# Mixture-of-experts results scattered by choice and token, the last two blocks added through TensorE, routing and mLSTM head mixing regrouped, in a two-model kernel on one core

## The reference

```
wmat = (q @ k^T) * exp(dmat - m_t)
num = wmat @ v + s_inter * (q @ c_st)
den = sum(wmat) + s_inter * (q @ n_st)
h = num / maximum(abs(den), floor)
```

```
for n in range(32):
    a, b = jnp.split(h @ w_up[n], 2, axis=-1)
    out = out + combine[:, n:n + 1] * ((jax.nn.silu(a) * b) @ w_down[n])
return x + out
```

## Time and profile before

| | |
|---|---|
| median of 3 runs | 2659.19 us |
| profiled execution | 2661.43 us, span 2659.4 us |
| PE busy | 2503.9 us (94%) |
| DVE busy | 1586.5 us (60%) |
| ACT busy | 1142.9 us (43%) |
| POOL busy | 235.2 us (9%) |
| head mixing | 457.9 to 534 us of the span |
| routing | about 2296 to 2312 us |
| expert blocks | 2312 to 2632.4 us, 32 blocks |
| combining | 2632.4 to 2659.4 us |

### The profile page before, as it was taken

The page is one execution under the profiler, slowest core; times in us unless marked ns, Lnnn a source line. Parts: engine busy times, 40 slices in busy tenths (PEclk is TensorE's granted clock), DMA queues, the critical chain, the costliest instruction groups (busy, mean ns, idle before and its releaser), DMA issues. The chain is left out here.

```text
span 2659.4 us, 32240 instructions
## 1 busy us (share of the span) xinstructions
PE 2503.9 (94%) x11395; PEld 1911.9 (72%) x11395; DVE 1586.5 (60%) x2344; ACT 1142.9 (43%) x1882; POOL 235.2 (9%) x239
## 2 busy tenths in 40 slices
PE   8999997699999999999999999999899999899995
PEld 6877785577888886766788888678757777666663
DVE  6766435645555535644555553547899645588884
ACT  5432332334444325623444442433332532377773
POOL 0000001000000000000000000355324000211111
PEclk9999999999999999999999999999999999799997
DMA  4321232032333321202333332323102013499995
GB/s 149 111 80 64 95 111 79 1 143 79 95 95 95 126 96 65 81 32 86 94 96 100 100 127 71 108 79 112 66 33 95 1 64 123 160 354 378 387 386 208
DMA packets 196719, 320.64 MB, mean 121 GB/s; under 512 B 16513, under 2 KB 112673, under 8 KB 196609
## 3 DMA queue, kind: packets, MB, share of 16 engines
q1 hardware_dynamic: 191678, 310.71, 33.8%
q0 software_dynamic: 4736, 8.40, 1.0%
q10 hardware_dynamic: 195, 0.06, 0.0%
HBM read 298.43 MB, written 29.10 MB: 123 GB/s over the span
## 5 line engine op out<-in xcount | busy, mean ns | idle before, releaser
L399 PE MATMUL ps<-ffn_parts 128*128 128x512 f32 x1056 | 411.6, 390 | 2.5 <-DVE ffn_parts L394 1.7
L401 PE MATMUL ps<-ffn_parts 128*128 128x512 f32 x1056 | 410.9, 389 | 0.0
L400 PE MATMUL ps<-ffn_parts 128*128 128x512 f32 x1056 | 410.8, 389 | 0.0
L399 PEld LDWEIGHTS ps<-ffn_parts 128*128 128x128 f32 x1056 | 198.2, 188 | 46.6 <-issue 2.6
L394 DVE TENSOR_TENSOR ffn_parts<-ring,ffn_parts 128x1024 fp32r<-128x1024 f32 x132 | 157.8, 1223 | 120.5 <-ACT ffn_parts L2437 107.4
L401 PEld LDWEIGHTS ps<-ffn_parts 128*128 128x128 f32 x1056 | 198.2, 188 | 41.2
L400 PEld LDWEIGHTS ps<-ffn_parts 128*128 128x128 f32 x1056 | 198.3, 188 | 40.9
L394 POOL TENSOR_TENSOR w_lo<-ring,w_hi 128x512 fp32r<-128x512 f32 (+1 forms) x112 | 159.9, 1432 | 721.1 <-ACT w_hi L558 720.8
L2488 DVE SCALAR_TENSOR_TENSOR y_tmp<-ps,pcol,y_tmp 128x511 f32<-128x511 f32 x88 | 61.9, 745 | 211.4 <-ACT y_tmp L2421 211.4
L1012 ACT CAST front_w_hi<-ring 128x512 fp32r<-128x512 f32 x104 | 64.1, 620 | 212.3 <-PE ps L401 212.2
L394 DVE TENSOR_TENSOR front_w_lo<-ring,front_w_hi 128x512 fp32r<-128x512 f32 x104 | 71.5, 689 | 129.8 <-ACT front_w_hi L1012 129.6
(11 more groups left out here) (669 smaller groups left out, 5638.7 us busy)
## 6 DMA issues: line engine op xcount, KB each, us to landing
ring<-in_w_up SPq DMA_DIRECT2D x32, 1536.0 KB, 8.8
ring<-in_ffn_w_up SPq DMA_DIRECT2D x88, 512.0 KB, 4.8
moe_down<-in_w_down SPq DMA_DIRECT2D x32, 1024.0 KB, 9.7
ring<-in_ab_w_in SPq DMA_DIRECT2D x13, 2048.0 KB, 7.9
ring<-in_w_in SPq DMA_DIRECT2D x11, 2048.0 KB, 7.8
ring<-in_ffn_w_down SPq DMA_DIRECT2D x10, 2048.0 KB, 7.7
ring<-in_w_up SPq DMA_DIRECT2D x32, 512.0 KB, 9.5
ring<-in_c_w_in SPq DMA_DIRECT2D x6, 2048.0 KB, 8.0
```

The lines of the kernel that those rows point to most:

```text
L399: nc.tensor.matmul(out, left[0], right[0], start=start, stop=False, **more)
L400: nc.tensor.matmul(out, left[0], right[1], start=False, stop=False, **more)
L401: return nc.tensor.matmul(out, left[1], right[0], start=False, stop=stop, **more)
```

## The change

**Head mixing.** Each direction gets two banks of its own (banks 0 and 1 for the first, 2 and 3 for the second), scores move to bank 4, and `SI` has one bank (5) instead of two. `sums` and `read_out` now work on one unit (4 chunks) and not on a head. The second direction's `read_out` adds directly into hm with four scalar_tensor_tensor of 128x128. DVE's order changes to prepare(n+1), finish(n-1).

**Routing.** DVE makes the rests of the first up block itself (before, POOL made two of three), ahead of `layout`; PE turns and multiplies block 0 before it waits for `placed`; there are more fill passes (1 more ahead, 1 before `tokens`, 5 before turn_rows(0), 2 before first(0)). POOL gathers blocks 0 to 3 before its other work. A second table, `result`, is computed like `token` (8 more small matmuls twice): for each row of a block, in which row of a 1024-row DRAM tensor `results_of_choices` (choice * 512 + token) its result belongs.

**Results.** SP's stores are gone. POOL scatters each block's results by an indirect DMA to their places (`hand_out`), except those of the last two blocks. While these two run, SP loads the 1024 rows back as 8 plain DMAs of 512 KB into the weights' ring, once POOL says it is free (`free_ring`). `slots_of_last` on DVE, `turn_shares` on PE and a copy on ACT make a table of shares by row of the last two blocks; `mixed` multiplies it with their results, 16 whole matmuls of 96x128 by 512, and DVE adds that and the loaded rows to x. The block end between the two parts, and `combine`, are gone. `rows_and_shares` is replaced by `shares_of_blocks`, after step 3.

The core of the diff (PE, ACT and DVE get the steps named above in their last two steps; left out with the tables' code):

```
             def mix(n):
                 h, d = units[n]
                 pe.wait_ge(*k.vb(n + 1))
-                if d == 0 and h >= 1:
-                    pe.wait_ge(*k.da(h))
+                if n >= 2:
+                    pe.wait_ge(*k.da(n - 1))
...
-            def read_out(h):
-                dve.wait_ge(*k.sb(h + 1))
...
+                dve.wait_ge(*k.sb(n + 1))
...
+                if d == 0:
+                    for tiles, values in nums(d):
+                        last = nc.vector.tensor_tensor(b.parts[:, tiles, :], values[:, :, 0:ML_D],
+                                                       spread(rden[:, tiles].rearrange("p (e o) -> p e o", o=1), [P, tiles.stop - tiles.start, ML_D]), ALU.mult)
+                else:
+                    for c in range(NT):
+                        last = nc.vector.scalar_tensor_tensor(out=hm[:, c, h * ML_D:(h + 1) * ML_D], in0=num(c, d)[:, 0:ML_D], scalar=rden[:, c:c + 1],
+                                                              in1=b.parts[:, c, :], op0=ALU.mult, op1=ALU.add)
+                last.then_inc(k.da.sem, 1)
                 dve.drain()
-                nc.vector.tensor_tensor(hm[:, :, h * ML_D:(h + 1) * ML_D], b.parts[:, 0:NT, :], b.parts[:, NT:2 * NT, :], ALU.add)
...
+            def finish(n):
+                h, d = units[n]
+                read_out(n)
+                if d == 1:
+                    gate(h)
+                    if h >= 1:
+                        mean(h - 1)
...
-            for n, (h, d) in enumerate(units):
+            for n in range(len(units)):
                 if n + 1 < len(units):
                     prepare(n + 1)
-                if d == 1:
-                    read_out(h)
-                    if h >= 1:
-                        mean(h - 1)
-                    dve.drain()
-                    gate(h)
+                if n >= 1:
+                    finish(n - 1)
+            finish(len(units) - 1)
...
-            def store(n):
-                sp.wait_ge(e.y_ready, at_block(n, 1, 1))
-                sp.dma_start(y_dram[bass.ds(at_block(n, ROWS), ROWS), :] if isinstance(n, tuple) else y_dram[n * ROWS:(n + 1) * ROWS, :],
-                             e.y[0:ROWS, side(n), :]).then_inc(e.y_ended if of_last_pair(n) else e.y_stored[side(n)], 16)
-
...
                     expert = expert_of(later(n, 2))
                     sp.wait_ge(e.up_split, at_block(n, SPLITS, SPLITS))
                     load_up(later(n, 2), expert, SPLIT_ROWS, e.up_loaded)
-                if inside(n, -2):
-                    store(later(n, -2))
...
-            store((before, 2, 4))
-            store((before, 3, 4))
-
-            sp.wait_ge(e.y_ended, 32)
+            for t in range(NT):
+                if t % 2 == 0:
+                    sp.wait_ge(*r.ring_free(t // 2 + 1))
+                for s in range(2):
+                    at = s * T + t * P
+                    sp.dma_start(picked[:, 2 * t + s, :], y_dram[at:at + P, :]).then_inc(r.row_picked[2 * t + s], 16)
+            for t in range(NT):
+                sp.wait_ge(*r.combined(t + 1))
+                sp.dma_start(tiles[:, t, :], k.x[:, t, :]).then_inc(k.param_loaded.sem, 16)
+            sp.wait_ge(*k.param_loaded(16 * NT))
...
+            def scatter(n, index):
+                nc.gpsimd.indirect_dma_start(y_dram, bass.IndirectOffsetOnAxis(ap=index, axis=0), e.y[0:ROWS, side(n), :], None, bounds_check=2 * T - 1, oob_is_err=False)\
+                    .then_inc(e.y_stored[side(n)], 16)
+
+            def hand_out(n):
+                s = side(n)
+                pool.wait_ge(e.y_ready, at_block(n, 1, 1))
+                if not isinstance(n, tuple):
+                    scatter(n, r.result[0:ROWS, n:n + 1])
+                    return
+                nc.gpsimd.tensor_copy(e.slot_result[0:ROWS, s:s + 1], r.result[0:ROWS, bass.ds(at_block(n), 1)])
+                pool.drain()
+                scatter(n, e.slot_result[0:ROWS, s:s + 1])
+
+            def gather_and_hand_out(n):
+                step(n)
+                if isinstance(n, tuple):
+                    hand_out(later(n, -2))
+                    return
+                hand_out(n - 4)
+                if n == STATIC_ROWS - 1:
+                    hand_out(n - 3)
+                    hand_out(n - 2)
+
+            def free_ring():
+                for s in range(2):
+                    pool.wait_ge(e.y_stored[s], pairs_before((before, 2, 4)))
+                for n in ((before, 2, 4), (before, 3, 4)):
+                    pool.wait_ge(e.up_split, at_block(n, SPLITS, SPLITS))
+                    pool.wait_ge(e.whole_done, at_block(n, 1, 1))
+                    nc.gpsimd.sem_inc(r.ring_free.sem, 1)
+
             def after(n):
...
-            step(0)
-            step(1)
-            after(1)
+            for n in range(4):
+                step(n)
+            after(3)
             before = pair_before_last(nc.gpsimd)
-            each_block(pool, before, lambda n: step(n) if isinstance(n, tuple) or n >= 2 else None, lambda n: after(n) if n > 1 else None, STATIC_ROWS)
+            each_block(pool, before, lambda n: gather_and_hand_out(n) if isinstance(n, tuple) or n >= 4 else None, lambda n: after(n) if n > 3 else None, STATIC_ROWS)
+            free_ring()
...
+            def turn_shares():
+                pe.wait_ge(*r.mix_built(1))
+                for b in range(2):
+                    for t in range(NT):
+                        last = nc.tensor.transpose(k.ps[0:ROWS, XB + b, t * P:(t + 1) * P], r.share_of_slot[:, 0, b, t, :], k.ident[:, :])
+                last.then_inc(r.mix_turned.sem, 1)
+
+            def mixed(t, b):
+                for half in range(2):
+                    last = nc.tensor.matmul(k.ps[:, MIXED[t] + half, :], r.slot_shares[0:ROWS, b, t * P:(t + 1) * P], e.y[0:ROWS, b, half * BANK:(half + 1) * BANK],
+                                            start=(b == 0), stop=(b == 1), skip_group_check=True)
+                if b == 1:
+                    last.then_inc(r.mixed.sem, 1)
+
+            fill_wait(k, NBANKS - 1, 4)
             pe.wait_ge(*r.rounded(2))
             ranks(0)
             counts(0)
             fill_wait(k, NBANKS - 1, 1)
             ranks(1)
             counts(1)
+            fill_wait(k, NBANKS - 1, 1)
             tokens(6, NE, in_first_blocks, r.token_of)
+            pe.wait_ge(*r.marked(3))
+            results(k.ps[0:ROWS, 5, 0:NE], r.token_of, r.result_of)
+            fill_wait(k, NBANKS - 1, 5)
+            turn_rows(0)
+            fill_wait(k, NBANKS - 1, 2)
+            first(0)
+            turn_rows(1)
```

240 lines of the change are left out of this document (131 added, 109 removed).

## The result

The change makes the kernel **slower**: 2818.99 us (median of 4 runs, 2817.09 to 2821.3) beside 2658.38 us for the kernel before on the same chip (4 runs), a ratio of 1.0602 with a 95% interval of 1.0587 to 1.0617. The forecast was 2757 us and its range ended at 2806: the direction was right, the size too small by 62 us.

What follows compares the result with a forecast made beforehand. PE was taken as the bound, busy for 94% of the span and without a gap in the expert blocks. Loop +118, end -10, routing -2 and +1, head mixing -9 give +98 on 2659.2: 2757 us, range 2688 to 2806.

Steps and rivals of the forecast that it cites:

- the ring: Expert loop: result, scatter, gather, landing, turning, result closes a ring of 14.4 us against 9.47 a block; 24 blocks, +118 us.
- POOL is early enough: Rival for the expert loop: the scatter's wait does not hold the gather back, PE keeps 9.47 us a block; 2639 us, chance 0.10.
- 0.98 for its issue, 0.30 between two indirect DMAs, then 1.10 (copy and start): Expert loop, POOL's way from the scatter's start to the gather's start, as three times in us.
- the landing: Expert loop: time from a gather's start until its rows land, taken as 5.0 us, plus 0.1 for PE's wake.
- the clock: Expert loop: PE idles 3 to 5 us a block, so half clock follows; taken as 1.0 us a block, 1.7 if always.
- The rule weighed in the forecast: Gather landing in the loop: 2.0 us plus bytes over 436 per ns gives 2.3 us, a ring of 11.7, a term of 54.
- The rival of the clock in every block: Expert loop: full 1.7 us of half clock and a landing of 6, ring 16.1 us; 2803 us, chance 0.22.
- head mixing: Head mixing stage: a head's new ring takes 8.2 us against 9.3; -9 us for 8 heads, bounds 0 and -15.
- the end: After the last result's copy starts on ACT: 18.2 us instead of 28.1, -10 us, bounds -12 and -3.
- routing: Routing and first block: block 0 no longer waits for `placed`; -2 us, from -4 to +3.5.
- the five fill passes at half clock: Routing, on PE: if the clock does not rise, five passes of 1.7 us end near 2315.3, 3.4 us later than now.

Runs made afterwards that it cites:

- e5: The change with a count (semaphore) in place of POOL's two drains between an index copy and its indirect DMA, in the loop: 2805.22 us, ratio 1.0544.
- e6: e1 with counts in place of POOL's two drains, so block n-4 is scattered behind the gather of block n: 2635.44 us, ratio 0.9905.
- e3: The change with five fill passes on PE ahead of each turning in the loop: 2808.15 us, ratio 1.0558.
- e10: e5 with five fill passes on PE before each turning in the loop: 2791.2 us, ratio 1.0489.
- e12: e10 with SP loading only 64 of the 1024 columns of each down weight in the loop: 2748.26 us, ratio 1.032.
- e1: The change with POOL scattering the result of four blocks before instead of two in the loop, drains kept: 2690.51 us, ratio 1.012.
- e4: The change with DVE's rests of the down weights and two thirds of the up weights cut to 16 columns in the loop: 2819.54 us, ratio 1.0595.
- e7: e6 with DVE's layout of the blocks ahead of the three rests of the first up block: 2635.19 us, ratio 0.99.

## Why the prediction was right or wrong

**Right: the ring.** Gathers start behind the results and are late in every block, PE stands for some 4.6 us at the turning; with the lag of four and without drains it is gone and the other parts show in full: 2635.4 us, where the rival "POOL is early enough" gave 2639. The lag of two is the cause: e5 and e6 differ in it alone, and by 170 us. What failed is the ring's length, 17.3 us instead of 14.4, in two of its terms.

**Wrong: the step "0.98 for its issue, 0.30 between two indirect DMAs, then 1.10 (copy and start)".** It priced POOL's way from the scatter to the gather at 2.38 us; it was 4.9 to 5.1 in the blocks shown, 4.7 to 7.4 over the loop. The 0.30 came from two gathers of the tail with no drain between them, and the 1.10 from a drain ahead of which nothing was in flight (the gather before it had started 9.5 us earlier and lands after 6.1). The trace could show neither the case of a drain behind a fresh indirect DMA nor its price; the bound I owed was the row I had, 6.1 us of landing. With 6.1 + 0.9 in place of 2.38 as an upper bound the ring of 14.4 would have reached 19.0 us, and a range up to there would have held the time.

**Wrong, but in the other direction: the landing.** I took 5.0 us and 0.1, it was 3.3 us in the median, 2.5 to 5.0 in all. It is not a constant, it goes with the moment of the gather among the loads: in e5, with a gather sooner by 2.9 us, it grew by 2.9. (The 7.3 given as the longest row of the saturated loop is a misreading: the earlier trace rows have 8.0. Nothing hung on it.) Of the pair of terms together, 2.38 + 5.1 = 7.5 forecast and 8.3 to 8.5 measured, only about 1 us was missing. That the sum was less wrong than its parts is luck: two errors of 2.7 and 1.8 us with opposite signs.

**Wrong in size: the clock.** "I take 1.0" for the half clock; from turning to the result's end it is 7.45 us against 4.70, so 2.75. Turning and most of the second product run at half clock (0.50 granted from 2568 to 2572), more than the 1.7 that I held for the most, and in most blocks; with fills it was 4.71 to 4.76 us (e3, e10, e12), so the 2.75 are the clock's. This is the larger part of the miss: (17.3 - 14.4) x 24 = 70 us, of which 1.75 x 24 = 42 by the clock and 1.05 x 24 = 25 by scatter and landing. The loop took 184.8 us more where 119 were forecast. e3 and e10 also show that the clock's term and the landing's cannot be added as I did: fills that kept the clock up shortened the 23 steps of the loop by 16 and 28 us, not by the 63 of 23 x 2.75, and a block's scatter or gather landed later in return.

**The rule weighed in the forecast**, that of the Trainium skill, "DMA: Bandwidth & Descriptors", "Anatomy of one DMA — SWDGE (gpsimd) path", 2.0 us plus the bytes for a landing: it gave 2.3 us here; 3.3 us in the ring, 6.2 in e5 and 6.8 for the scatters of e6, in the median, say again that the load of the DMA engines decides.

**The rival of the clock in every block** (2803) had one of the two causes right; it came near by a landing of 6 us, which was 3.3, and had no wait between scatter and gather either.

**The small parts** stood in their numbers: head mixing -9.7 (forecast -9), the end -10.0 (-10), routing -3.4 (-2). In head mixing the number came by another way than the shorter reading out that I counted: PE waits for that as long as before (13.6 against 13.3 us), and the gain lies in the waits between the scores and DVE's product. For the five fill passes at half clock I took 1.7 us each, where the earlier trace rows give 1.9; the clock was up (five passes in 4.54 us), so nothing hung on it. The table's "all other code" of -3.0 is unchanged code; some 2 us of it are 16 small matmuls just ahead of the routing (3.63 against 1.98 us), which ran at a granted clock of 0.50 before and of 1.00 here.

## What to carry to other kernels

A drain on POOL is no cheap ordering of a copy ahead of a DMA once another indirect DMA is in flight: it waits for that DMA's landing, so order the two by a count. Put a scatter so many blocks behind that no gather has to wait for its result, and look at POOL's order of issue when a second indirect DMA joins the loop. And when a ring has two holds at about the same time (here a drain and the loads beside the gather), taking one away shows nearly nothing: try both together before calling either innocent.

## What of the hardware was unexpected

- The drain itself: with nothing in flight 0.9 us, behind a gather of some 7 us landing 7.00 us, and with a count instead 0.86 to 0.89 us [e1 and e6].
- POOL against DVE on their SBUF port: a scatter's issue takes 1.97 us beside the rests of 128x1024 on DVE and 0.94 with rests of 16 columns, an index copy 0.37 against 0.20 (e4); the first gather of the changed kernel took 3.7 us to issue beside three rests, and 1.21 in e7 with the rests behind it. The Trainium skill, "SBUF — State Buffer", "A bandwidth-pool intuition that's wrong (but worth ruling out)", tells of a DMA issued from GpSimd that waits beside a DVE tensor_copy, since its descriptors can't be written until DVE lets the shared port go. The rests here are no tensor_copy but subtractions with two operands in SBUF; the runs agree in that POOL's issue is held, and they don't show by which port. No run here shows a cost of it in time.
- The same 96-row gather landed after 2.7, 3.3, 5.4 or 6.2 us in the median of 2450 to 2600 us, in e3, the change, e6 and e5. What differs is the moment of its issue among the weights' loads and how close these stand.
